# Inverse square roots of all norms on ScalarE: exp(-ln/2) in place of a square root and a VectorE reciprocal

## The reference, cut to what matters

```python
def rms_norm(x, g):                      # each layer's input, the final norm, each head of the first attention
    y = xf * lax.rsqrt(jnp.mean(xf * xf, axis=-1, keepdims=True) + NORM_EPS)
def l2_norm(x):                          # q and k of the delta rule, per head
    return xf * lax.rsqrt(jnp.sum(xf * xf, axis=-1, keepdims=True) + EPS)
o_a = rms_norm_2(o_a, gdn_norm_gain[l])  # each of 8 delta heads
qb = rms_norm_2(q_b.reshape(B, T, SWA_HEADS, SWA_HEAD_DIM), q_norm_gain[l])
kb = rms_norm_2(k_b.reshape(B, T, SWA_KV_HEADS, SWA_HEAD_DIM), k_norm_gain[l])
```

## Time and profile before

| | |
|---|---|
| median of 3 runs | 4302.54 us (4299.52 to 4306.98) |
| span of the profiled execution | 4304.2 us |
| PE busy | 4128.5 us, 96% |
| DVE busy | 2440.3 us, 57% |
| ACT busy | 807.5 us, 19% |
| mean granted TensorE clock | 0.980 |
| reciprocals of 128x512 | 54, 180.7 us |
| activation table loads | 160, 205.3 us |

### The profile page before, as it was taken

One profiled execution on the slowest core, in us unless ns is written; L12 is line 12 of the kernel. 1 busy time (PEld: TensorE's weight loads), 2 busy tenths in 40 slices (PEclk: granted clock), 3 DMA queues, 4 the chain that ended last, 5 costly groups with the idle time before them and its releaser, 6 DMA issues.

```text
span 4304.2 us, 41305 instructions
## 1 busy us (share of the span) xinstructions
PE 4128.5 (96%) x16042; PEld 2766.0 (64%) x16042; DVE 2440.3 (57%) x4211; ACT 807.5 (19%) x1450; POOL 498.5 (12%) x816
## 2 busy tenths in 40 slices
PE   6899999999999999999999999999999999999999
PEld 3565544444447555444468568878788877787888
DVE  6576436674533564366666466465655367666643
ACT  2222201131011221011311122121211122230000
POOL 0233111111202231111111000000000101100000
PEclk7999999999999999999999999999999999999999
DMA  9633333334552333332444332222121333434433
GB/s 311 204 118 105 108 122 108 121 124 146 151 166 73 105 113 115 121 121 93 130 142 152 113 102 70 64 69 64 61 73 59 92 104 115 126 98 137 137 103 103
DMA packets 370192, 499.29 MB, mean 116 GB/s; under 512 B 44379, under 2 KB 279118, under 8 KB 369486
## 3 DMA queue, kind: packets, MB, share of 16 engines
q1 hardware_dynamic: 289984, 340.16, 24.5%
q0 software_dynamic: 38608, 125.86, 9.2%
q10 hardware_dynamic: 41406, 30.63, 2.2%
HBM read 462.51 MB, written 34.08 MB: 115 GB/s over the span
## 4 chain that ended last, share of the span: by engine, by line
PE 82%; DVE 12%; ACT 2%; DMA 2%; issue 1%; ACTq 0%; POOL 0%; DVEq 0%; SPq 0%
PE bank L108 80%; DVE tring L132 2%; DVE tring L117 2%; PE bank L111 2%; DVE tring L123 2%; DMA side<-in_w_ada 1%; ACT tring L114 1%; DVE wring L117 1%; DVE dring L120 1%; DVE bank L117 1%; DVE tring L120 1%; DVE dring L117 0%; ACT L114 0%; DVE region_b L117 0%; DVE sring L138 0%
## 5 line engine op out<-in xcount | busy, mean ns | idle before, releaser
L108 PE MATMUL bank<-region_b,wring 128*128 128x256 f32 (+2 forms) x4448 | 1322.8, 451 | 7.8 <-ACT region_b L114 6.6
L108 PE MATMUL bank<-region_a,wring 128*128 128x256 f32 (+1 forms) x3232 | 1083.5, 489 | 29.1 <-DVE wring L117 29.1
L108 PEld LDWEIGHTS bank<-region_b,wring 128*128 128x128 f32 (+1 forms) x4448 | 830.2, 190 | 412.5 <-issue 332.3
L108 PEld LDWEIGHTS bank<-region_a,wring 128*128 128x128 f32 x3232 | 613.8, 194 | 416.2 <-issue 337.8
L147 POOL DMA_DIRECT2D side<-in_w_ada x384 | 209.0, 545 | 1309.9 <-DVE tring L123 951.7
L123 DVE SCALAR_TENSOR_TENSOR tring<-side,cact,tring 128x512 f32<-128x512 f32 x360 | 303.2, 842 | 78.1 <-DMA side<-in_w_ada 42.3
L108 PE MATMUL bank<-wring,region_b 128*128 128x512 f32 (+1 forms) x640 | 265.5, 572 | 10.7 <-ACT region_b L114 10.7
L114 ACT ACT_TABLE_LOAD x160 | 205.3, 1283 | 354.2 <-DVE sring L120 283.8
L117 DVE TENSOR_TENSOR tring<-bank,tring 128x256 f32<-128x256 f32 (+1 forms) x229 | 101.0, 441 | 299.6 <-PE bank L108 296.2
L117 DVE TENSOR_TENSOR wring<-wring 128x1024 f32<-128x1024 f32 (+1 forms) x213 | 234.8, 1102 | 17.4 <-PE bank L108 8.5
L108 PE MATMUL bank<-wring,region_a 128*128 128x512 f32 x512 | 226.8, 601 | 6.0 <-ACT region_a L114 6.0
(11 more groups left out here) (285 smaller groups left out, 4320.6 us busy)
## 6 DMA issues: line engine op xcount, KB each, us to landing
wring<-in_w_in SPq DMA_DIRECT2D x180, 1024.0 KB, 5.3
side<-in_w_ada POOLq DMA_DIRECT2D x384, 256.0 KB, 3.2
wring<-in_w_out SPq DMA_DIRECT2D x48, 1024.0 KB, 8.2
yaT<-in_w_ada SPq DMA_DIRECT2D x16, 1024.0 KB, 9.4
wring<-in_w_glu SPq DMA_DIRECT2D x16, 1024.0 KB, 7.7
tring<-x_saved SPq DMA_DIRECT2D x48, 256.0 KB, 2.9
gring<-in_w_ada POOLq DMA_DIRECT2D x43, 256.0 KB, 3.0
SS<-in_w_ada SPq DMA_DIRECT2D x8, 1024.0 KB, 9.8
```

The costliest lines, as they stand in the source:

```text
L108: return self.e.matmul(*a, **k) if self.e else self
```

## The change

ScalarE now computes ln(scale * sum + eps) out of the bank, and then exp(-0.5 * that) in place, in a second instruction that waits for the first. VectorE's reciprocals of these tiles and the semaphore `rooted` are gone; `root_ready` is now raised by ScalarE, and `head_out`, `d_out`, `unit`, `k_unit` and `q_unit` wait for it. A helper keeps account of the table set as the program is built, and loads a set that holds both functions where another one is in place. Where the set is in place from an earlier root, exponentials in between (softmaxes) use it too.

```diff
-    def activation(self, *a, **k):
-        return self.e.activation(*a, **k) if self.e else self
+    def activation(self, o, x, f, **k):
+        if f not in (ACT.Copy, ACT.Identity, ACT.Square, ACT.Abs) and (f, self.table) != (ACT.Exp, "log"):
+            self.table = "log" if f == ACT.Ln else "other"
+        return self.e.activation(o, x, f, **k) if self.e else self
+
+    def preload(self, name):
+        if self.e:
+            self.e.preload_act_table_set(name)
...
             do("root_sum", "delta", h)
             aux.give("root", "delta", h)
             yield
-            do("root_invert", "delta", h)
             do("d_out", h)
...
-            def root_invert(*key):
-                r = root_spec(*key)[4]
-                dve.wait_ge(*rooted.of(*key))
-                dve.reciprocal(r, r).then_inc(*root_ready.up(*key))
-
...
             def d_out(h):
+                dve.wait_ge(*root_ready.of("delta", h))
                 tt(dq(h, ORAW), dq(h, ORAW), dq(h, LO), M)
...
+            def log_table():
+
+                if act.table != "log":
+                    act.preload("natural_log_exp_and_others")
+                    act.table = "log"
+
+            def inverse_root(o, src, bank, scale, shift, *event):
+
+                log_table()
+                act.activation(o, src, ACT.Ln, bias=shift, scale=scale).then_inc(*a_step.up())
+                if bank:
+                    aux.leave(bank, act.mine())
+                own()
+                act.activation(o, o, ACT.Exp, scale=-0.5).then_inc(*root_ready.up(*event))
+
             def norm_root(l):
                 room(temps.clear("r", l))
                 act.wait_ge(*(summed.of("norm", 0, KT - 1) if l == 0 else summed.of("rsq", 0)))
-                act.activation(temps.at("r", l), aux.at("norm", l)[:, :], ACT.Sqrt, bias=eps, scale=1.0 / D).then_inc(
-                    *rooted.up("norm", l))
-                aux.leave(("norm", l), act.mine())
+                inverse_root(temps.at("r", l), aux.at("norm", l)[:, :], ("norm", l), 1.0 / D, eps, "norm", l)
...
             def root_sum(*key):
                 _, _, _, scale, sq = root_spec(*key)
                 act.wait_ge(*summed.of(*key))
-                act.activation(sq, aux.at("root", *key)[:, :], ACT.Sqrt, bias=eps, scale=scale).then_inc(*rooted.up(*key))
-                aux.leave(("root", *key), act.mine())
+                inverse_root(sq, aux.at("root", *key)[:, :], ("root", *key), scale, eps, *key)
```

More of the change, by code:

```diff
@@ L92, in __init__ @@
     def __init__(self):
-        self.e, self.reached, self.newest = None, {}, None
+        self.e, self.reached, self.newest, self.table = None, {}, None, None
     def wait_ge(self, sem, value):
@@ L409, in build @@
         taken_d = sem("taken_by_dve", dve)
-        root_ready = sem("root_ready", dve)
+        both_ready = sem("both_norms_ready", dve)
+        scaled_x = sem("x_scaled", dve)
         ssm_d = sem("ssm_by_dve", dve)
@@ L417, in build @@
         a_step = sem("act_step", act)
+        root_ready = sem("root_ready", act)
         x_ready_a = sem("x_ready_by_act", act)
         squared = sem("squared", act)
-        rooted = sem("rooted", act)
         h_ready = sem("h_ready", act)
@@ L591, in root_of @@
             yield
-            do("root_invert", *key)
         def modulation(m):
@@ L2135, in sum_square @@
                     temps.leave((name, l, n), dve.mine())
[L2137 to L2140, removed]
             def norm_roots():
@@ L2148, in norm_roots @@
                 own()
-                dve.scalar_tensor_tensor(both, aux.at("norm", 2)[:, :], 1.0 / D, both, M, AD).then_inc(*root_ready.up("both"))
+                dve.scalar_tensor_tensor(both, aux.at("norm", 2)[:, :], 1.0 / D, both, M, AD).then_inc(*both_ready.up())
                 aux.leave(("norm", 2), dve.mine())
[L2151 to L2157, removed]
             def norm_scale(l, k):
@@ L2399, in values @@
                 aux.leave(("val", l, h), dve.mine())
-            def root_invert(*key):
-                r = root_spec(*key)[4]
-                dve.wait_ge(*rooted.of(*key))
-                dve.reciprocal(r, r).then_inc(*root_ready.up(*key))
             def head_out(l, h):
                 raw_, r, ya = temps.at("raw", l, h), temps.at("root", "head", l, h), lay[l]["yaT"]
+                dve.wait_ge(*root_ready.of("head", l, h))
                 tt(raw_, raw_, r, M)
@@ L2867, in norm_root @@
                 act.wait_ge(*(summed.of("norm", 0, KT - 1) if l == 0 else summed.of("rsq", 0)))
-                act.activation(temps.at("r", l), aux.at("norm", l)[:, :], ACT.Sqrt, bias=eps, scale=1.0 / D).then_inc(
-                    *rooted.up("norm", l))
-                aux.leave(("norm", l), act.mine())
+                inverse_root(temps.at("r", l), aux.at("norm", l)[:, :], ("norm", l), 1.0 / D, eps, "norm", l)
             def norm_roots():
-                act.wait_ge(*root_ready.of("both"))
-                act.activation(temps.at("both", 2), temps.at("both", 2), ACT.Sqrt).then_inc(*rooted.up("both"))
+                act.wait_ge(*both_ready.of())
+                inverse_root(temps.at("both", 2), temps.at("both", 2), None, 1.0, 0.0, "norm", 2)
             def final_root():
@@ L2878, in final_root @@
                 act.wait_ge(*summed.of("rsq", 1))
-                act.wait_ge(*root_ready.of("both"))
-                act.activation(temps.at("r", 2), aux.at("norm", 3)[:, :], ACT.Sqrt, bias=eps, scale=1.0 / D).then_inc(*rooted.up("final"))
-                aux.leave(("norm", 3), act.mine())
+                act.wait_ge(*both_ready.of())
+                inverse_root(temps.at("r", 2), aux.at("norm", 3)[:, :], ("norm", 3), 1.0 / D, eps, "final")
             def x_store(l):
@@ L3428, in build @@
         for p in (pe, dve, act, pool, sp):
-            p.reached, p.newest = {}, None
+            p.reached, p.newest, p.table = {}, None, None
         block = ctx.enter_context(nc.Block())
```

12 lines of the change are left out of this document (6 added, 6 removed).

## The result

The changed kernel takes 4235.2 us (median of 4 runs, 4231.2 to 4236.4) against 4302.9 for the kernel before (4299.5 to 4307.0) on the same chip: a ratio of 0.9841, with a 95% interval of 0.9829 to 0.9852. That is 67.8 us less; 61.1 were forecast. The profiled execution has a span of 4234.6 us and a mean granted clock of 0.987 (0.980 before).

The account below looks back on a forecast made before the run. TensorE, busy 96% of the span, bounds the kernel, so only its waits count. 29.0 + 12.7 + 3.5 + 16.1 + 1.4 + 2.7 - 4.3 = 61.1 us off the median 4302.5 gives 4241 us, range 4224 to 4276.

Parts of the forecast that it names:

- Weight sums: TensorE's waits for VectorE's sums of weights (wring), 31.4 us in all, would lose 29.0 us.
- Window softmax and logits: In the window attention, TensorE's waits for the scaled softmax and window logits would lose 12.7 us.
- First attention: Four waits standing behind a reciprocal in the first attention would give 3.5 of 12.6 us.
- Clock: Slow matmuls behind long stalls, at pair ends and in five other places, would go with those stalls: 16.1 us.
- Norm before layer two: TensorE waits for this root itself; gain 1.4 us, not 2.7, because the table load now carries the sum's wait.
- Norm before block two: The combined table set is already loaded here; from root to scale 4.05 us becomes 0.7 + 0.66, gain 2.7.
- First norm: VectorE gets 3.35 us here, but the modulation weights' DMA feeds the stage; between 0 and 3.35, taken as 0.
- Debit: Exps ahead of squares TensorE waits for, at the second key norm and in conv stages, would cost 4.3 us.
- Rival A: Other waits step in at the stalls, each losing one reciprocal, not two, and the clock dips as before: 4276; chance 0.15.
- B: All reciprocals on the chain that ended last were worth their time, 86 us less the debit: 4221; chance 0.08.
- C: ScalarE takes the reciprocal's place, slower: weight sums wait for DMA, TensorE meets the Exp at most roots: 4338; chance 0.02.
- D: Nothing measurable: weight sums, window softmax and clock fail because of DMA; norms, attention and debit remain: 4299; chance 0.02.

Follow-up runs that it names:

- e11: Changed kernel with the old Sqrt and reciprocal at the first layer norm alone; 4235.6 us.
- e10: Changed kernel with the table load ahead of the wait and the Exp one plan step late for q, k and key tiles, timed again; 4226.1 us.
- e1: Kernel with the new root in the 8 delta heads only, the other 46 norms keeping Sqrt and reciprocal; 4275.8 us, against 4302.1 for the kernel before.
- e2: Kernel with the new root only in the second head of each delta pair (4 norms), the others keeping Sqrt and reciprocal; 4289.8 us, ratio 0.9969 to the kernel before.
- e6: Changed kernel with the explicit table load ahead of the wait for the sum of squares at all roots; 4230.2 us.
- e9: Changed kernel unaltered, timed again in one series with later runs; 4233.1 us.
- e4: Kernel with the new root at the first layer norm alone, all other norms keeping Sqrt and reciprocal; 4298.4 us, ratio 0.9992 to the kernel before.
- e7: Changed kernel with the Exp one plan step later for 16 delta-rule q and k tiles and 2 key tiles, after the next square; 4228.9 us.
- e5: Changed kernel with 23 table loads put back (160 in all), each ahead of the wait that follows it; 4236.1 us.
- e3: Kernel before with all Sqrts and 160 loads kept, no reciprocal or Exp, tiles scaled by a constant; 4225.1 us, ratio 0.9818.

## Why the prediction was right, step by step

Direction, time and range held: 4235.2 lies 5.8 below 4241 and inside 4224 to 4276. By its steps:

1. Weight sums: 27.4 went, not 29.0. The pair ends kept 0.55 each, where the forecast had let 6.16 go whole. The missing part is in another row: TensorE's waits for ScalarE's dring, just ahead of those ends, fell from 4.3 to 2.4, so 27.4 + 1.9 = 29.3 in all.
2. Window softmax and logits: 12.7 forecast, 13.0 + 1.5 - 1.8 = 12.7 measured.
3. First attention: 3.5 forecast, 12.6 - 7.8 = 4.8 measured. The four waits that I had counted gave 3.5 as forecast; two of 0.66 and 0.68, which I had not counted among those behind a reciprocal, went as well.
4. Clock: 16.1 forecast; PE's busy time in block two fell by 1799.64 - 1783.67 = 16.0. To agree within 0.1 is luck: that busy time is between 1780.7 (e11) and 1785.0 (e10) in profiles with the same roots there, and in e1 the clock gave 5.5 of 7.8. In e2 the term stayed behind stalls of 3.7 and more and was absent behind 2.11.
5. Norm before layer two: stall forecast at 4.6, measured 4.45. That the load carries the wait is shown by e6: with the load ahead of the wait the stall is 3.26.
6. Norm before block two: 3.9 forecast, 3.89 measured. The stretch ahead of it also has 1.3 less busy time, which is scatter: its last six sums of squares take 4.54 us in the kernel before and 2.84 after the change, but 4.54 again in e9, the same changed kernel, and 2.84 in e4, which has the old root there.
7. **First norm: this is the step that failed.** "The stage is fed by the modulation weights' DMA", so nothing was taken. The DMA is busy there (share 0.96 up to 156 us), but TensorE stood still for 4.92 at the first product that this norm feeds, a stall that the prediction did not look at, and the refills behind it wait for a slot that VectorE has to free. A queue that is busy nearly always can still be paced by who frees its slots. Both moved: the stall fell to 1.44, and the refill is issued 3.6 earlier (means of 44.2 and 40.6 behind the first sum). By the thirteen profiles the start keeps 3.9 of it, e4 is 3.7 faster and e11 2.5 slower, so the term was near 3.35 and not 0. The rest of the 6.7 in the profiled pair is not the change's as far as the runs show: 1.3 lies ahead of the norm, where the transposes ran at a slower clock before, and the remaining 1.5 is less than the two profiles of the changed kernel differ by there (126.2 and 123.5).
8. Debit: 4.3 forecast; PE's waits for ScalarE's tring rose by 22.4 - 17.8 = 4.6, in the conv stage before the delta heads by 0.76 + 0.49 + 0.49 = 1.7 (forecast 1.7), in three others by 0.74, and at the key norm by 0.66. e7 takes 3.9 of them back by moving the Exp behind the square. The loads at nothing: e5 holds that to one to three microseconds.

Rival A (the next wait steps in) would have left 2 to 3 us with a dip at the pair ends; they have 0.5 and no dip, and e1 with e2 shows that the second reciprocal gives as much as the first. B (4221) is ruled out as a mechanism: unrounded, the chain counts the reciprocals at 2.1%, 90 us. In e3, where nothing at all replaces them, the profiled span is 80.3 shorter, and only 55.4 of these are TensorE's idle time (175.7 before, 120.3 there); the other 24.9 are clock, which the chain does not tell of. Its number was not far off because many of these reciprocals did stand ahead of something that TensorE wanted, and because the clock, which it left out, made up for part of the rest. C and D fell with the first trace.

## What to carry to other kernels

A slow instruction can cost more by what stands behind it in its engine's queue than by what waits for its own result. To price its removal, find the stalls of the bounding engine whose releaser is late behind it, and take the smaller of the stall and the time removed; add the slow clock behind long stalls. In a stage that DMA feeds, read the bounding engine's stalls as well, and ask who frees the slot that a DMA refills, even where the queue looks full. When a replacement goes to another engine, put its second half behind whatever the bounding engine needs from there first, and put a table load ahead of the wait and not behind it.

## What the runs showed of the hardware that was not expected

A VectorE reciprocal of 128x512 in float32 takes 3346 ns, where a product of the same tile takes 690; Ln and Exp take 687 and 630 on ScalarE, the second starting 0.02 to 0.03 us after the first's end. The Trainium skill (ScalarE: Activation LUTs, What it computes) advises VectorE's reciprocal and a Sqrt for an inverse root, in place of ScalarE's own inverse root, which has known accuracy issues. By these rows that is the dearer way for a full tile when VectorE has other work queued; how accurate Ln and Exp are, no run here compares.

A stall of 2.11 us left the next 16 matmuls at 3.72 us; stalls of 3.7 to 4.1 had 5.41 behind them, one of 5.31 had 5.25, and three of 6.2 had 5.94, 5.58 and 5.57. The time lost behind these stalls hardly grows with their length.

At layer two in e6 an ACT_TABLE_LOAD holds up ScalarE for its 1283 ns and nothing more: the activation behind it starts 0.01 us after its end (1260.47 + 1.28, then 1261.76). The Trainium skill (ScalarE: Activation LUTs, What ACT_TABLE_LOAD costs) adds a drain of about 1380 ns to the load for every switch to a different set. It does not show here: this load changes the set, and no gap ahead of it or behind it is longer than 0.02 us. The 23 loads of e5 reload the set that is in place, so they say nothing on a switch.
